# Dividing the on-chip memory anew in a two-layer hybrid attention and mixture-of-experts trunk

## The reference

```python
z = x @ w_in                                   # 1024 -> 6656 columns: 7 projections and 3 gates
ya, yb, yc = chunked attention, pooling mixer, differential attention
merged = sigmoid(ga)*(ya@w_a) + sigmoid(gb)*(yb@w_b) + sigmoid(gc)*(yc@w_c)
x = layer_norm(ALPHA*x + merged @ w_out)       # first norm
idx, wts = route(x)                            # 8 of 64 experts for each token
y = sum over chosen experts of (silu(x@w_gate)*(x@w_up)) @ w_down * gate  +  shared expert
x = layer_norm(ALPHA*x + y)                    # second norm
```

## Time and profile before

| | us |
|---|---|
| median of three runs | 1477.59 |
| profiled execution | 1476.62 |
| its span | 1474.8 |
| TensorE busy in the span | 1431.4 (97%) |
| VectorE busy | 550.0 |
| ScalarE busy | 464.3 |
| expert stage of layer 0, first up matmul to last scatter | about 273 to 739 |
| expert stage of layer 1, likewise | about 1006 to 1463 |

### The profile page before, as it was taken

How to read it: one execution, slowest core, us unless ns; L and a number is a source line. 1 busy time by engine, 2 the same in 40 slices (tenths; PEclk the granted TensorE clock), 3 DMA queues, 4 the chain that set the end, 5 groups by cost and what they waited for, 6 DMA issues and landing times.

```text
span 1474.8 us, 23850 instructions
## 1 busy us (share of the span) xinstructions
PE 1431.4 (97%) x10104; PEld 868.9 (59%) x10104; DVE 550.0 (37%) x882; ACT 464.3 (31%) x745; POOL 32.8 (2%) x30
## 2 busy tenths in 40 slices
PE   8999999999999999989899999999999999999995
PEld 8999998544444444334289999984334334333441
DVE  4577756221221221111355678562121221221224
ACT  5565544222122221112335745432222222211212
POOL 0011000000000000000001110000000000000000
PEclk9999999999999999999999999999999999999998
DMA  9653459899999999999925544588999999999994
GB/s 307 201 202 128 167 181 416 320 426 424 426 424 426 424 426 424 421 424 425 382 93 169 188 167 154 200 366 360 425 424 426 423 427 423 427 424 426 424 426 155
DMA packets 80692, 497.76 MB, mean 338 GB/s; under 512 B 6416, under 2 KB 11792, under 8 KB 47568
## 3 DMA queue, kind: packets, MB, share of 16 engines
q1 hardware_dynamic: 78304, 492.61, 82.5%
q10 hardware_dynamic: 2288, 3.67, 0.7%
HBM read 493.90 MB, written 1.05 MB: 336 GB/s over the span
## 4 chain that ended last, share of the span: by engine, by line
PE 81%; DMA 14%; ACT 2%; DVE 2%; issue 1%; SPq 0%; DVEq 0%
PE bank L1711 27%; PE bank L1536 17%; PE bank L1739 12%; PE bank L1656 6%; DMA arena<-in_expert_w_gate_up 6%; PE bank L1685 4%; DMA gu_a<-in_expert_w_gate_up 4%; DMA ring_w<-in_w_in 4%; PE bank L1601 3%; PE bank L1491 3%; PE bank L1429 2%; ACT w_hi L712 1%; PE bank L1725 1%; PE bank L1677 1%; PE bank L1574 1%
## 5 line engine op out<-in xcount | busy, mean ns | idle before, releaser
L943 DVE TENSOR_TENSOR w_lo<-ring_w,w_hi 128x2048 fp32r<-128x2048 f32 x71 | 162.4, 2289 | 106.6 <-ACT w_hi L712 106.3
L1536 PE MATMUL bank<-x_hi,w_hi 128*128 128x256 f32 x704 | 201.0, 286 | 1.0 <-ACT arena L778 0.7
L1536 PE MATMUL bank<-x_hi,w_lo 128*128 128x256 f32 x704 | 199.2, 283 | 0.0
L1536 PE MATMUL bank<-x_lo,w_hi 128*128 128x256 f32 x704 | 199.2, 283 | 0.0
L1346 DVE SCALAR_TENSOR_TENSOR y_lo<-bank,slot_info,y_hi 128x512 fp32r<-128x512 f32 x128 | 96.1, 751 | 206.0 <-ACT y_hi L859 206.0
L1332 DVE TENSOR_TENSOR hid<-hid,bank 128x256 f32<-128x256 f32 x64 | 27.0, 421 | 388.6 <-ACT hid L842 388.6
L842 ACT ACTIVATE hid<-bank 128x256 f32<-128x256 f32 x64 | 24.6, 384 | 430.7 <-PE bank L1711 430.7
L859 ACT ACTIVATE y_hi<-bank,slot_info 128x512 fp32r<-128x512 f32 x128 | 88.0, 687 | 222.2 <-PE bank L1739 222.1
L712 ACT CAST w_hi<-ring_w 128x2048 fp32r<-128x2048 f32 x71 | 135.0, 1903 | 52.4 <-PE bank L1601 30.5
L1536 PEld LDWEIGHTS bank<-x_hi,w_hi 128*128 128x128 f32 x704 | 135.0, 192 | 3.2 <-ACT arena L778 1.5
L1536 PEld LDWEIGHTS bank<-x_lo,w_hi 128*128 128x128 f32 x704 | 135.1, 192 | 0.1
(11 more groups left out here) (218 smaller groups left out, 1906.2 us busy)
## 6 DMA issues: line engine op xcount, KB each, us to landing
arena<-in_expert_w_gate_up SPq DMA_DIRECT2D x24, 4096.0 KB, 22.7
gu_a<-in_expert_w_gate_up SPq DMA_DIRECT2D x24, 4096.0 KB, 21.8
ring_w<-in_expert_w_gate_up SPq DMA_DIRECT2D x32, 2048.0 KB, 22.4
ring_w<-in_w_in SPq DMA_DIRECT2D x25, 2048.0 KB, 8.6
arena<-in_expert_w_down SPq DMA_DIRECT2D x24, 2048.0 KB, 21.6
dn_a<-in_expert_w_down SPq DMA_DIRECT2D x24, 2048.0 KB, 19.6
dn_c<-in_expert_w_down SPq DMA_DIRECT2D x16, 2048.0 KB, 23.1
ring_w<-in_w_out SPq DMA_DIRECT2D x4, 2048.0 KB, 8.0
```

The source lines that it names most:

```text
L943: v.tensor_tensor(chunk_part(w_lo, n), chunk_in(n), chunk_part(w_hi, n).bitcast(F32), ALU.subtract).then_inc(w_lo_ready, 1)
L1536: ins = mm(b[:, S * c:S * c + S], lhs, rhs, start=(k == 0 and a + w == 0), stop=(k == KD - 1 and a == 1))
```

## The change

All of it is a new map of the on-chip memory and what follows from it for the order of loads.

- The up weights of slot 0 (`gu_a`) move into the arena, where `xg_hi`, `xg_lo`, one buffer of gathered tokens and `y_hi` were. The up weights of slot 2 (`gu_c`) move from the ring to the weights region, where those of slot 0 were. The down weights of slot 2 (`dn_c`) move to half 0 of the ring; the odd buffer of gathered tokens, `x_t` and `y_hi` move to half 1. `xg_hi` and `xg_lo` lie where `x_hi` and `x_lo` are. `y_lo`, the gate tiles `sig`, the router's scratch and the parameters of both norms (now two tiles) share the region of `xe_even`.
- Pair 1's up weights are issued behind block 14, after a new wait for `y_lo_ready_of[2]`; its down weights behind block 15. They were issued behind `merged_ready`, after block 18.
- Pair 0's up weights are issued after `merged_lo_ready`, ahead of block 19; they waited for `h_ready`. Its down weights still do, and behind them come now the up weights of pair 2, which waited for the shared expert in two halves. The down weights of pair 2 wait for `shared_up_done` and no longer stand behind `shared_down` and the router's count.
- The up weights of slot 2 come in one DMA of 4 MB in place of two of 2 MB.
- Block 0 of the next layer waits for the down matmuls of pair 23 in place of its up matmuls. Block 1 waits until all scatters of the layer are done (`acc_done`); it waited for nothing but the loads ahead of it and the freeing of its half.
- Chunk 2 of the next layer is no longer split in the step of pair 31, but behind the last transpose of x (task `("xt", 0, 3)`).

```diff
+FIRST_UP = 14
...
-        gu_a = place("gu_a", 0, [P, 2, KD, 2 * FE])
+        gu_c = place("gu_c", 0, [P, 2, KD, 2 * FE])
         dn_a = place("dn_a", 32 * KB, [P, 2, KF, D])
...
-        x_t = place("x_t", 0, [P, KD, S])
+        xg_hi = place("xg_hi", 0, [P, TT, KD, P], F32R)
+        xg_lo = place("xg_lo", 8 * KB, [P, TT, KD, P], F32R)
+        place = region("ring_region", 32 * KB)
+        ring_w = place("ring_w", 0, [P, 2, 4096])
         dn_c = place("dn_c", 0, [P, 2, KF, D])
+        xe_odd = place("xe_odd", 16 * KB, [P, KD, 2 * WIDE * SLOTS])
+        x_t = place("x_t", 24 * KB, [P, KD, S])
+        y_hi = place("y_hi", 28 * KB, [P, D], F32R)
+        place = region("xe_region", 16 * KB)
+        xe_even = place("xe_even", 0, [P, KD, 2 * WIDE * SLOTS])
+        sig = place("sig", 0, [P, KD, S])[:]
+        ln_gb = [place("ln1_gb", 8 * KB, [P, 2, D]), place("ln2_gb", 0, [P, 2, D])]
+        y_lo = place("y_lo", 12 * KB, [P, D], F32R)
...
-        gu = [gu_a[:], gu_b, ring_w[:].rearrange("p e (k n) -> p e k n", k=KD)]
+        gu_a = view(12288, 2, KD, 2 * FE)
+        gu = [gu_a, gu_b, gu_c[:]]
...
+                    if n == FIRST_UP:
+                        sp.wait_ge(y_lo_ready_of[2], l + 1)
+                        load_up(l, 1, 1)
+                    if n == FIRST_UP + 1:
+                        load_down(l, 1, 1)
                 load_block(l, NB - 2)
-                sp.wait_ge(merged_ready, 4 * (l + 1))
-                load_up(l, 1, 1)
-                load_down(l, 1, 1)
+                sp.wait_ge(merged_lo_ready, 4 * (l + 1))
+                load_up(l, 0, 0)
                 load_block(l, NB - 1)
                 sp.wait_ge(h_ready, 2 * TT * (l + 1))
-                load_up(l, 0, 0)
                 load_down(l, 0, 0)
+                load_up(l, 2, 2)
                 sp.wait_ge(shared_up_done, 2 * (l + 1))
-                load_up(l, 2, 2, (0, 1))
-                sp.wait_ge(shared_down, l + 1)
-                load_up(l, 2, 2, (1, 2))
+                load_down(l, 2, 2)
                 more = more_rounds(sp, l)
-                load_down(l, 2, 2)
...
                 if l + 1 < L:
-                    sp.wait_ge(up_done, 2 * start + SHORT_FROM - 2)
+                    sp.wait_ge(y_done, 2 * (2 * start + SHORT_FROM - 2))
                     load_block(l + 1, 0)
...
                 if l + 1 < L:
+                    sp.wait_ge(acc_done, 2 * TT * (l + 1))
                     load_block(l + 1, 1)
...
-                        if l == 0 and j == 3:
-                            for u in range(WBUFS):
-                                split_high(0, u)
+                        if j == 3:
+                            for u in range(0 if l == 0 else 2, WBUFS):
+                                split_high(l, u)
...
-                    if last and odd and l + 1 < L:
-                        split_high(l + 1, 2)
...
+                        elif j == 3:
+                            split_low(l, 2)
...
-                    if last and l + 1 < L:
-                        split_low(l + 1, 2)
...
-                    pe.wait_ge(gu_in[slot], (32 if slot == 2 else 16) * loads)
+                    pe.wait_ge(gu_in[slot], 16 * loads)
```

More of the change, by code:

```diff
@@ L195, in sem @@
             return ctx.enter_context(nc.semaphore(name))
-        ring_w = sb("ring_w", [P, 2, 4096])
         x_tok = sb("x_tok", [P, TT, D])
@@ L232, in build @@
         onehot = sb("onehot", [P, TT, 2 * WIDE * HALF], F32R)
-        y_lo = sb("y_lo", [P, D], F32R)
         onehot_t = sb("onehot_t", [P, P], F32R)
@@ L255, in build @@
         x_lo = place("x_lo", 8 * KB, [P, KD, S], F32R)
-        x_t = place("x_t", 0, [P, KD, S])
+        xg_hi = place("xg_hi", 0, [P, TT, KD, P], F32R)
+        xg_lo = place("xg_lo", 8 * KB, [P, TT, KD, P], F32R)
+        place = region("ring_region", 32 * KB)
+        ring_w = place("ring_w", 0, [P, 2, 4096])
         dn_c = place("dn_c", 0, [P, 2, KF, D])
[L258 to L266, removed]
+        xe_odd = place("xe_odd", 16 * KB, [P, KD, 2 * WIDE * SLOTS])
[6 more added lines that the diff above has]
+        y_lo = place("y_lo", 12 * KB, [P, D], F32R)
+        score = place("score", 12 * KB, [P, TT, NE])
+        choice = place("choice", 12 * KB + 512, [P, TT, NE])
+        replaced = place("replaced", 13 * KB, [P, TT, NE])
+        sel = place("sel", 13 * KB + 512, [P, TT, NE])
+        top = place("top", 14 * KB, [P, TT * GROUPS, 8])
+        beats = place("beats", 14 * KB + 512, [P, TT, GROUPS, GROUPS])
+        ties = place("ties", 15 * KB, [P, TT, GROUPS, GROUPS])
+        sh_silu = sb("sh_silu", [P, KF, S])[:]
+        sh_t = sb("sh_t", [P, KF, S])[:]
         arena_at = (nc.sbuf_base + 31) // 32 * 32
@@ L287, in build @@
         dn_b = view(8192, 2, KF, D)
[L288 to L295, removed]
-        gu = [gu_a[:], gu_b, ring_w[:].rearrange("p e (k n) -> p e k n", k=KD)]
+        gu_a = view(12288, 2, KD, 2 * FE)
+        xe_t = [xe_even[:], xe_odd[:]]
+        gu = [gu_a, gu_b, gu_c[:]]
         dn = [dn_a[:], dn_b, dn_c[:]]
@@ L307, in build @@
         yb_t = view(2048, KW, S)
-        sig = view(0, KD, S)
         merged = view(18432, KD, S)
@@ L495, in load_ln @@
             g, b = ((ln1_g, ln1_b), (ln2_g, ln2_b))[which]
-            eng.dma_start(ln_gb[:, 0, :], g[l].partition_broadcast(P)).then_inc(ln_in, 16)
-            eng.dma_start(ln_gb[:, 1, :], b[l].partition_broadcast(P)).then_inc(ln_in, 16)
+            eng.dma_start(ln_gb[which][:, 0, :], g[l].partition_broadcast(P)).then_inc(ln_in, 16)
+            eng.dma_start(ln_gb[which][:, 1, :], b[l].partition_broadcast(P)).then_inc(ln_in, 16)
         def load_bias(eng, l):
@@ L556, in load_block, with load_up @@
                 sp.dma_start(dst, src).then_inc(block_in[slot], 16)
[L558 to L565, removed]
+            def load_up(l, slot, pair):
+                sp.dma_start(gu[slot], expert_w_gate_up[l, bass.ds(2 * pair, 2)]
                              .rearrange("e (p k) n -> p e k n", k=KD)).then_inc(gu_in[slot], 16)
@@ L1014, in norm_apply @@
                                                     scalar=moments[:, 1:2] if by_act else mean_var[:, t, 0:1],
-                                                    in1=ln_gb[:, 0, cols], op0=ALU.add if by_act else ALU.subtract,
+                                                    in1=ln_gb[which][:, 0, cols], op0=ALU.add if by_act else ALU.subtract,
                                                     op1=ALU.mult))
@@ L1021, in norm_apply @@
                         v.scalar_tensor_tensor(out=row[:, cols], in0=row[:, cols], scalar=rstd[:, t:t + 1],
-                                               in1=ln_gb[:, 1, cols], op0=ALU.mult, op1=ALU.add
+                                               in1=ln_gb[which][:, 1, cols], op0=ALU.mult, op1=ALU.add
                                                ).then_inc(normed if which else ln_done, 1)
```

## The result

The changed kernel took 1468.70 us (median of four runs, 1467.38 to 1469.81) against 1477.20 us (four runs of the kernel before). The ratio is 0.9947, 95% interval 0.9935 to 0.9959: 7.8 us faster, between 6.1 and 9.6 (the two medians lie 8.5 us apart). The forecast was 1470.8 us and 6.8 us faster. The profiled execution took 1469.81 us, with a span of 1468.0 us, 6.8 us under that of before.

What follows compares the result with a forecast made beforehand. TensorE, 97% busy, was taken to bound the kernel until the full DMA queue sets the late expert stage; 4.2 + 2.9 + 0.5 - 0.8 = 6.8 us gave 1470.8 us, 8-in-10 range 1466.0 to 1474.6.

Steps and rivals of the forecast that it cites:

- The early loads move only the moment at which the DMA engines become continuously busy: Expert stages: pair 3's up weights land sooner after an unchanged issue, gaining 1.9 + 2.3 us, together 4.2 us (1.6 to 10.2).
- the 12.9 us for 4 MB into an empty queue: Expert stage: pair 3's up weights land 12.9 us after issue, where it was 14.8 and 15.2 us.
- The z stage pays 0.8 us: Loads ahead of block 16 (`w_out`): 0.5 us to spare in layer 0, 0.8 us late in layer 1; ends 0 and -4.4.
- The end of layer 0, 2.9 us: Pair 31's step: without chunk 2's split, `y_lo` follows the down matmuls after 1.3 us, not 4.2; gain 2.9 (2.5 to 3.5).
- The matmuls of no use and behind, 0.5 us, at most 1.1: Behind layer 0's last `y_lo`: these matmuls may run at 2.4 GHz, until VectorE's norms decide; gain 0.5 us (0 to 1.1).
- Chunk 2 at the transition costs nothing: Start of layer 1: chunk 2's cast and subtraction end at 757.4 us, 1.5 us before z task 2; 0 paid.
- The four terms: Early loads 4.2, end of layer 0 2.9, matmuls of no use 0.5, z stage -0.8: 6.8 us.
- The rival of a w_out late enough to lose: Z stage: loads ahead of block 16 delay the out projection, making the kernel slower, 1487.7 us; chance 0.06.
- The rival by which all 17.5 us vanish: Expert stages: all of TensorE's waits for late up weights go, giving 1457.5 us; chance 0.03.
- The rival by which the queue had no share: Expert stages: pair 3 lands as before, only the end of layer 0 gains, 1475.0 us; chance 0.07.
- The rival with 11.6 us for 4 MB: Expert stages: start-up near 2.0 us, so pair 3 lands sooner still, gains 3.2 + 3.6, 1468.2 us; chance 0.09.

## Why the prediction was right, and where it missed

The time lies in the range, 2.1 us under the forecast, and the mechanisms were those named. By the prediction's own steps:

- *The early loads move only the moment at which the DMA engines become continuously busy.* Right: pair 3 landed sooner after its issue, and 2 MB more lengthened both stages by 5 us. The size was off: 2.7 us for 4.2. The term at fault is the 12.9 us for 4 MB into an empty queue, made of block 14's 7.9 us and 4.97 us; the chip showed 13.5 and 13.4, a gain of 1.3 + 1.8 = 3.1 us. The last landing moved by 0.4 us less than that, about as much as a stretch repeats.
- *The z stage pays 0.8 us.* Right in kind, too small: 1.9 us. The term is the transfers of layer 0, 9.93 us for pair 1's up weights behind block 14 first of all. Block 14 landed at 173.5 + 7.9 = 181.4, pair 1's up weights at 174.6 + 17.9 = 192.5: 11.1 us. Block 16 was not 0.5 us early there but held the cast up by 1.07 us. In layer 1 the same load took 9.8 us, and block 16 held the cast up by 0.96 us, near the 0.8 forecast.
- *The end of layer 0, 2.9 us.* Measured 2.9, in two profiles in which the clock fell in pair 31's up matmuls. Where it doesn't fall the move is worth more, 4.9 us (above), which the prediction didn't consider.
- *The matmuls of no use and behind, 0.5 us, at most 1.1.* Measured 1.7, outside its bounds. The bound counted the time after which VectorE's norms decide, and held one share of it (the norms end 13.2 us after the last `y_lo` began, where it was 14.2). It left out that the last transposes had waited for products which were themselves late: the time from the end of the norms to z task 2 went from 7.5 to 6.8 us. The eleven profiles tie it to the clock; the run with fewer matmuls of no use doesn't settle it, since its clock was lower for longer.
- *Chunk 2 at the transition costs nothing.* Right: its cast ran at 746.6 to 748.5, the subtraction to 750.8, and z task 2 began at 752.1.
- The four terms as measured give 2.7 + 2.9 + 1.7 - 1.9 = 5.4 us of the 6.8 us between the profiles; 1.6 us lie ahead of the first moved load and 0.2 us against. The misses of the terms (-1.5, -1.1, +1.2) cancel only in part, and 1.4 us are left. That the profiles differ by just the 6.8 us forecast is luck: it takes the 1.6 us that aren't of the change. The 7.8 us of the ratio are not accounted for term by term.
- The rival of a w_out late enough to lose has its mechanism here, at 1.9 us where the rival had 17.7. The rival by which all 17.5 us vanish is refuted by the 14.4 us that stay. The rival by which the queue had no share is refuted by the landings. The rival with 11.6 us for 4 MB has a slip in its price: 3.2 + 3.6 + 3.4 - 0.8 is 9.4 us, not 10.0, and 1468.2 us follows from the 9.4. That is nearer to the measured 1468.7 than my 1470.8, but its mechanism is refuted by the landings. With 13.4 us for 4 MB the estimate of 11.6 us, worked out from the Trainium skill (DMA: Bandwidth & Descriptors, Anatomy of one DMA), is further off than mine; that section is on DMAs issued from GpSimd, these are from SyncE.

## What to carry to other kernels

Where a stream of transfers is continuous, weights loaded earlier help only by what they take out of the queue at the first recurring load, here about 3 us; look as well for bytes that stand ahead of the last needed ones and can wait. Here that was the norm's parameters, some 3 us by my estimate; block 0's place alone gave nothing that could be told from noise, since what it won in the queue was lost again in pair 31's step. A load put ahead of another in one queue delays it by all its bytes, and a chunk without slack there costs at once. Where a large rearrangement carries a small reordering with it, run the small one alone: here it was 4.6 of the 5.4 us that the stretches give the change, and all of it by the ratios.

## What the runs showed of the hardware

Pair 31's 32 up matmuls take 7.09 us or 8.8 us with the same operands, by the clock granted while they run. The clock is 1.00 throughout in the first case and 0.81 in the mean in the second, because it falls to 0.50 for some 3 us in between. Idle time ahead of them and their duration in layer 0, changed kernel and the one with the down weights behind `w_out`:

```profile
716.29 8.78 PE L1713 MATMUL bank<-arena,xe_odd 128*64 128x512 f32 x32 [2.23 <-DMA arena<-in_expert_w_gate_up]
```
```profile
716.27 7.09 PE L1713 MATMUL bank<-arena,xe_odd 128*64 128x512 f32 x32 [0.38 <-DMA arena<-in_expert_w_gate_up]
```

The weights land at 716.2 us in both. In the second kernel the clock had been low for longer behind the wait for pair 26 (0.68 for 1.00 in the mean from 645 to 650 us), TensorE came from pair 30 1.8 us later and had less idle time. It is tempting to take the shorter idle time for the reason, but layer 1 shows that it isn't enough of one. The changed kernel and the one with no expert load in the z stage:

```profile
1438.81 8.78 PE L1713 MATMUL bank<-arena,xe_odd 128*64 128x512 f32 x32 [2.84 <-DMA arena<-in_expert_w_gate_up]
```
```profile
1436.29 7.09 PE L1709 MATMUL bank<-arena,xe_odd 128*64 128x512 f32 x32 [2.82 <-DMA arena<-in_expert_w_gate_up]
```

In the 4.3 us ahead of them TensorE was busy for 1.46 and 1.48 us at a clock of 1.00 in both, and yet the clock fell in one and not in the other. What decides it is not shown by any run here. Such a 1.7 us comes and goes in kernels that differ elsewhere, and a comparison of single executions has to take it out first.

A 4 MB load in a continuous queue takes 9.9 us, and 13.3 to 13.8 us into an empty queue. Directly behind a lone 2 MB load its last byte came 11.1 us after the other's in layer 0 and 9.8 us after it in layer 1, where the 2 MB had taken 9.1 us in place of 7.9; from issue to landing it took 17.9 and 17.8 us.
